# Four u tile buffers and a new order of loads, one-hots and selections in a one-core encoder step

## The reference

```
x += W_o [ headRMS(DiffAttn(x_n)) ; headRMS(StickBreak(x_n)) ]
h  = x;  xb = RMSNorm(h)                       # feed-forward part, "PEER"
q  = (xb @ w_q) as 8 heads x 2 halves x 128    # scores against 128 sub keys per half
top 16 of each half, top 16 of the 256 sums  -> 16 experts per head, gate = softmax
y  = sum over 128 chosen experts of gelu(u[e] . xb) * gate * v[e]
```

## Time and profile before

| what | value |
|---|---|
| time, median of 3 runs | 2113.67 us (2110.81 to 2116.14) |
| the profiled execution's own time | 2118.96 us |
| its span, first to last instruction | 2117.2 us, 25395 instructions |
| mean granted TensorE clock | 0.958 |
| PE busy | 1952.6 us, 92% |
| DVE busy | 1276.0 us, 60% |
| ACT busy | 653.5 us, 31% |
| POOL busy | 516.1 us, 24% |
| DMA | 484.30 MB, mean 229 GB/s |
| chain that ended last | PE 57%, DMA 20%, DVE 13%, ACT 6%, issue 3% |

### The profile page before, as it was taken

How to read it: one execution, slowest core, us unless ns; L and a number is a source line. 1 busy time by engine, 2 the same in 40 slices (tenths; PEclk the granted TensorE clock), 3 DMA queues, 4 the chain that set the end, 5 groups by cost and what they waited for, 6 DMA issues and landing times.

```text
span 2117.2 us, 25395 instructions
## 1 busy us (share of the span) xinstructions
PE 1952.6 (92%) x9365; PEld 1470.9 (69%) x9365; DVE 1276.0 (60%) x2475; ACT 653.5 (31%) x1392; POOL 516.1 (24%) x408
## 2 busy tenths in 40 slices
PE   6999899999999898998898989779999999999997
PEld 6998665589998788887887888764444444444443
DVE  3113775633767676888998778554545554465456
ACT  3223564433444333335676667220000000000001
POOL 0001100000000121222122223444444444354441
PEclk9999798779999999999999999889999999999999
DMA  5223000002123687776777788989999999999996
GB/s 193 85 81 130 24 1 1 1 23 70 61 81 117 213 264 254 261 246 209 236 252 244 261 300 303 367 304 360 354 375 353 360 379 343 375 371 336 386 351 228
DMA packets 168351, 484.30 MB, mean 229 GB/s; under 512 B 15200, under 2 KB 72544, under 8 KB 164528
## 3 DMA queue, kind: packets, MB, share of 16 engines
q1 hardware_dynamic: 111280, 270.92, 35.9%
q0 software_dynamic: 56528, 208.28, 27.5%
q10 hardware_dynamic: 432, 3.64, 0.4%
HBM read 422.61 MB, written 59.90 MB: 228 GB/s over the span
## 4 chain that ended last, share of the span: by engine, by line
PE 57%; DMA 20%; DVE 13%; ACT 6%; issue 3%; SPq 1%; POOL 0%; ACTq 0%; DVEq 0%; POOLq 0%
PE ps L903 23%; DMA raw<-w_tiles 11%; PE ps L555 10%; PE ps L884 7%; PE ps L822 5%; DMA g_in<-gates_scattered 4%; DMA act_in<-activated 4%; DVE w_lo L1176 3%; DVE hot L1518 3%; PE ps L649 3%; ACT hot L1114 2%; ACT w_hi L1138 2%; PE ps L573 2%; PE ps L640 1%; PE ps L690 1%
## 5 line engine op out<-in xcount | busy, mean ns | idle before, releaser
L903 PE MATMUL ps<-v_buf,p_ring 128*128 128x512 f32 x1536 | 662.4, 593 | 17.3 <-DVE p_ring L1583 14.7
L903 PEld LDWEIGHTS ps<-v_buf,p_ring 128*128 128x128 f32 x1536 | 291.1, 190 | 388.0 <-issue 363.8
L884 PE MATMUL ps<-md_hi,w_hi 128*128 128x384 f32 x1024 | 367.5, 359 | 61.2 <-DVE w_lo L1176 59.9
L1176 DVE TENSOR_TENSOR w_lo<-raw,w_hi 128x1024 fp32r<-128x1024 f32 x176 | 215.5, 1224 | 329.6 <-ACT w_hi L1138 182.6
L884 PE MATMUL ps<-md_lo,w_hi 128*128 128x384 f32 x1024 | 351.5, 343 | 0.0
L884 PE MATMUL ps<-md_hi,w_lo 128*128 128x384 f32 x1024 | 351.2, 343 | 0.0
L535 POOL DMA_INDIRECT ring<-u_rows,idx_a x128 | 173.7, 1357 | 598.5 <-DVE dots L1536 478.1
L1583 DVE TENSOR_TENSOR p_ring<-act_in,g_in 128x384 f32<-128x384 f32 x128 | 70.6, 553 | 318.0 <-DMA act_in<-activated 208.5
L884 PEld LDWEIGHTS ps<-md_hi,w_hi 128*128 128x128 f32 x1024 | 199.3, 195 | 77.4 <-DVE w_lo L1176 76.4
L1544 DVE SCALAR_TENSOR_TENSOR acc<-ring,actg,acc 128x1024 f32<-128x1024 f32 x188 | 232.9, 1277 | 0.8 <-DMA ring<-v_rows,idx_a 0.8
L1536 DVE CUSTOM_DVE_ANT_0 ring<-ring,x_n 128x1024 f32<-128x1024 f32 x192 | 230.0, 1220 | 1.8
(11 more groups left out here) (230 smaller groups left out, 2509.4 us busy)
## 6 DMA issues: line engine op xcount, KB each, us to landing
raw<-w_tiles SPq DMA_DIRECT2D x176, 512.0 KB, 5.3
v_buf<-v_rows SPq DMA_DIRECT2D x128, 512.0 KB, 8.4
activated<-act_st SPq DMA_DIRECT2D x128, 192.0 KB, 2.6
gates_scattered<-g_st SPq DMA_DIRECT2D x24, 1024.0 KB, 5.0
g_in<-gates_scattered SPq DMA_DIRECT2D x32, 768.0 KB, 15.4
act_in<-activated SPq DMA_DIRECT2D x32, 768.0 KB, 12.0
kv_t<-qkv ACTq DMA_DIRECT2D x3, 1184.0 KB, 7.5
xh<-x_t SPq DMA_DIRECT2D x8, 296.0 KB, 13.2
```

The source lines that it names most:

```text
L884: mm = nc.tensor.matmul(ps[:, slot, 0:ND], w[:, slot, kc, :], x[:, kc, :], start=(kc == 0 and j == 0), stop=(kc == KC - 1 and j == 2))
L903: mm = nc.tensor.matmul(ps[:, 2 + 2 * t + h, :], p_ring[:, i % 3, t * P:(t + 1) * P], v_buf[i % V_SLOTS][:, 512 * h:512 * h + 512], start= ...
L1176: TT(w_lo[:, slot], raw[:, slot], w_hi[:, slot].bitcast(F32), SUB).then_inc(w_split, 1)
```

## The change

- `raw_u`: four buffers for u tiles. The two new ones lie where buffers 5 and 6 of the ring were, so the ring has 5 buffers for the first 139 gathers (`RING_U`, `RING_AT`) and 7 after; the first use of buffers 5 and 6 waits for the end of the u stage (`u_done`).
- `load_u`: SP issues the load of tile i+4, not i+2, at the head of tile i's turn. The first loads of the new buffers wait for the last sub-key scores (`sc_done`).
- DVE's order per tile is one-hots, remainder, step, dots; ACT's is cast, scaling, copies, gelu.
- `act_dram` holds four tiles side by side, so `load_acts` reads 6 KB per partition in one row; the stores stay 1.5 KB per partition.
- Six selections of D2 move into the query stage, one in each of its last six tiles (`D2_EARLY`). Three "sel" steps fewer remain (74 steps, not 77), and `STEP_LINE` has 54 steps before tile 64, not 55. The exponents now stand at tiles 8, 31, 49, 66 and 89.

```diff
-SEL_STEPS, TOP_STEPS = {RT_B: 4, RT_D2: 8}, 13
+D2_EARLY = 6
+SEL_STEPS, TOP_STEPS = {RT_B: 4, RT_D2: (16 - D2_EARLY) // 2}, 13
-STEP_LINE = [(0, 0), (9, 13), (64, 55), (90, N_STEPS)]
+STEP_LINE = [(0, 0), (9, 13), (64, 54), (90, N_STEPS)]
-RING = 7
+RING_U, RING_V, RING_AT = 5, 7, U_DOTS
+RAW_SLOTS = 4
-    act_dram = nc.dram_tensor("activated", (N_EXP * P, ND), F32).ap()
+    act_dram = nc.dram_tensor("activated", (N_EXP // 4 * P, 4 * ND), F32).ap()
+        raw_u = [raw[:, 0], raw[:, 1]] + [at(f"raw{k}", [P, KC, P], F32, region + 8192 + 4096 * (k - 2))[:] for k in (2, 3)]
-        def ring_slot(s):
-
-            return ring[s % RING][:], gath_in[s % RING], 16 * (s // RING + 1)
+        ring_slots, last_use, landings = [], [None] * RING_V, [0] * RING_V
+        for op in range(N_OPS):
+            k = op % RING_U if op < RING_AT else (op - RING_AT) % RING_V
+            landings[k] += 1
+            ring_slots.append((k, 16 * landings[k], last_use[k]))
+            last_use[k] = op
...
             def load_acts(grp):
-                sp.dma_start(act_in[:, grp % 2], act_dram[4 * grp * P:4 * (grp + 1) * P, :].rearrange(
-                    "(j p) t -> p j t", p=P)).then_inc(act_in_s[grp % 2], 16)
+                sp.dma_start(act_in[:, grp % 2].rearrange("p j t -> p (j t)"),
+                             act_dram[grp * P:(grp + 1) * P, :]).then_inc(act_in_s[grp % 2], 16)
...
+            def load_u(i):
+                if i < RAW_SLOTS:
+                    sp.wait_ge(sc_done, N_PQ)
+                else:
+                    sp.wait_ge(w_split, B_U + i - RAW_SLOTS + 3)
+                sp.dma_start(raw_u[i % RAW_SLOTS], w_tiles[(B_U + i) * P:(B_U + i + 1) * P, :]).then_inc(
+                    raw_in[i % RAW_SLOTS], 16)
+
+            for i in range(2, RAW_SLOTS):
+                load_u(i)
             for i in range(N_EXP):
-                if i + 2 < N_EXP:
-                    load_tile(B_U + i + 2, i % 2)
+                if i + RAW_SLOTS < N_EXP:
+                    load_u(i + RAW_SLOTS)
...
-                if s >= RING:
-                    pool.wait_ge(gath_used, s - RING + 1)
+                if before is not None:
+                    pool.wait_ge(gath_used, before + 1)
+                if before is None and slot >= RING_U:
+                    pool.wait_ge(u_done, N_EXP)
...
+                for g in groups_of(i, 0):
+                    scale_hots(g)
                 for g in groups_of(i, 1):
                     take_gates(g)
-                for g in groups_of(i, 0):
-                    scale_hots(g)
...
                     select([(s, u - 1) for s in EARLY])
+                if u >= N_PQ - D2_EARLY:
+                    select([(RT_D2, u - N_PQ + D2_EARLY)])
...
             for i in range(N_EXP):
+                for g in groups_of(i, 0):
+                    one_hot(g)
                 if i + 1 < N_EXP:
-                    lo_part(B_U + i + 1, (i + 1) % 2)
+                    lo_part(B_U + i + 1, (i + 1) % 2, raw_u[(i + 1) % RAW_SLOTS])
```

More of the change, by code:

```diff
@@ L236, in bass_hybrid_step @@
         ring_off = [m0_off + 2 * KC * ND * 4 + 4096 * k for k in range(3)] + [region + 4096 * k for k in range(4)]
-        ring = [at(f"ring{k}", [P, D], F32, ring_off[k]) for k in range(RING)]
+        ring = [at(f"ring{k}", [P, D], F32, ring_off[k]) for k in range(RING_V)]
+        raw_u = [raw[:, 0], raw[:, 1]] + [at(f"raw{k}", [P, KC, P], F32, region + 8192 + 4096 * (k - 2))[:] for k in (2, 3)]
         mq_hi = at("mq_hi", [P, KC, TQ], F32R, region)
@@ L314, in bass_hybrid_step @@
         tables_in, caches_in = sem("tables_in"), sem("caches_in")
-        raw_in = [sem("raw_in0"), sem("raw_in1")]
+        raw_in = [sem(f"raw_in{k}") for k in range(RAW_SLOTS)]
         hi_ready = sem("hi_ready")
@@ L347, in bass_hybrid_step @@
         idx_ready = sem("idx_ready")
-        gath_in = [sem(f"gath_in{k}") for k in range(RING)]
+        gath_in = [sem(f"gath_in{k}") for k in range(RING_V)]
         gath_used, gl_done, gl_gated = sem("gath_used"), sem("gl_done"), sem("gl_gated")
@@ L441, in _ @@
                 sp.wait_ge(act_done, i + 1)
-                sp.dma_start(act_dram[i * P:(i + 1) * P, :], act_st[:, i % 4]).then_inc(act_stored[i % 4], 16)
+                sp.dma_start(act_dram[i // 4 * P:(i // 4 + 1) * P, i % 4 * ND:(i % 4 + 1) * ND],
+                             act_st[:, i % 4]).then_inc(act_stored[i % 4], 16)
                 if i == G_AT + 2:
@@ L530, in _ @@
                     pool.wait_ge(idx_ready, 2)
-                dst, landed, _ = ring_slot(s)
-                if s >= RING:
-                    pool.wait_ge(gath_used, s - RING + 1)
+                slot, _, before = ring_slots[s]
+                if before is not None:
+                    pool.wait_ge(gath_used, before + 1)
+                if before is None and slot >= RING_U:
+                    pool.wait_ge(u_done, N_EXP)
                 idx = idx_b[:, k:k + 1] if blk else idx_a[:, k:k + 1]
-                pool.indirect_dma_start(dst, None, u_rows if table == "u" else v_rows,
-                                        bass.IndirectOffsetOnAxis(ap=idx, axis=0)).then_inc(landed, 16)
+                pool.indirect_dma_start(ring[slot][:], None, u_rows if table == "u" else v_rows,
+                                        bass.IndirectOffsetOnAxis(ap=idx, axis=0)).then_inc(gath_in[slot], 16)
         @block.tensor
@@ L1132, in _ @@
                 if i + 1 < N_EXP:
-                    act.wait_ge(raw_in[n % 2], 16 * (n // 2 + 1))
+                    k = (i + 1) % RAW_SLOTS
+                    act.wait_ge(raw_in[k], 16 * ((B_U // 2 if k < 2 else 0) + (i + 1) // RAW_SLOTS + 1))
                     if i == 0:
@@ L1137, in _ @@
                         act.wait_ge(u_done, i)
-                    nc.scalar.copy(w_hi[:, n % 2], raw[:, n % 2]).then_inc(hi_ready, 1)
+                    nc.scalar.copy(w_hi[:, n % 2], raw_u[k]).then_inc(hi_ready, 1)
                 if 1 <= i <= 10:
@@ L1172, in _, with lo_part @@
             TT, TS = nc.vector.tensor_tensor, nc.vector.tensor_scalar
-            def lo_part(n, slot):
+            def lo_part(n, slot, src=None):
                 dve.wait_ge(hi_ready, n + 1)
-                TT(w_lo[:, slot], raw[:, slot], w_hi[:, slot].bitcast(F32), SUB).then_inc(w_split, 1)
+                TT(w_lo[:, slot], raw[:, slot] if src is None else src, w_hi[:, slot].bitcast(F32), SUB).then_inc(w_split, 1)
             def factors(name, w, r=1):
@@ L1480, in routing @@
                         for k in range(SEL_STEPS[s]):
-                            select([(s, 2 * k), (s, 2 * k + 1)])
+                            h0 = 2 * k + (D2_EARLY if s == RT_D2 else 0)
+                            select([(s, h0), (s, h0 + 1)])
                             yield None
@@ L1524, in gathered @@
                 table, blk, k = OPS[s]
-                rows, landed, n = ring_slot(s)
+                slot, n, _ = ring_slots[s]
+                rows = ring[slot][:]
                 if s == 0:
@@ L1533, in gathered @@
                     dve.wait_ge(gl_gated, 1)
-                dve.wait_ge(landed, n)
+                dve.wait_ge(gath_in[slot], n)
                 if table == "u":
@@ L1563, in _ @@
                     normed_rows()
-                for g in groups_of(i, 0):
-                    one_hot(g)
                 for _ in range(along(STEP_LINE, i), along(STEP_LINE, i + 1)):
```

## The result

The changed kernel took **2019.07 us** (median of 4 runs, 2013.59 to 2027.12), the kernel before 2114.9 us in the runs beside it (median of 4, 2110.81 to 2117.15). Between the two profiled executions (2118.96 and 2013.59 us) the difference is 105.4 us.

A forecast was written before the change was run, and what follows sets the result against it. PE was 92% busy, with 120 us of the u stage not its own work, mainly late loads and scaling. Terms 15 + 18 + 14 + 7 + 3 = 57 us gave 2057 us for the median, range 2032 to 2085 us.

The forecast's parts named there:

- the corner where everything works at once: Whole kernel: every part reaches its upper end; left out of the range, with two rivals, together less than 0.2.
- First stretch: Tiles 12 to 63: four u buffers remove most pauses from late loads, -15 us, bounds 8 and 22.
- Second stretch: Tiles 64 to 89: new orders and three steps fewer, with DVE the limit, -18 us, bounds 6 and 27.
- Third stretch: Tiles 90 to 111: one-hots ahead and loads on time remove PE's pauses, -14 us, bounds 8 and 20.
- Last stretch: Tiles 112 to 127: limited by transfers at some 365 GB/s, -7 us, bounds 0 and 18.
- Rows of 6 KB: V stage: longer rows for activations land little sooner, -3 us of 0 to 14.7.
- New waits: Waits added by `load_u`, the first loads and POOL's wait for the u stage's end: 0 us.
- Selections in the query stage: Query stage: six moved selections fit into DVE's waits for ACT's scores, 0 us; without that cover 10 us.
- DVE did not take the loads' place: Rival, first two stretches: pauses and idle time come back as DVE's, gain 38 us, 2076 us; chance 0.17.
- the rival with 0.12: V stage: longer pieces get more of the engines and pauses go, -14.7 instead of -3, 2045 us; chance 0.12.
- The ring of five did not starve DVE: Rival, last two stretches: five gather buffers starve DVE, slower, 2131 us at 20 us landing; chance 0.03.
- Loads did come earlier: Denies the rival that transfers limit the u stage and two more buffers only queue, 2086 us; chance 0.06.

The follow-up runs named there:

- early preload: The changed kernel with gate pieces issued at v tiles 1, 3, 5, 7 and 3.1 MB of v-stage preloads moved to tiles 94 to 106; 2000.26 us.
- ring of three: The changed kernel with three gather buffers in the u stage instead of five; 2022.75 us, one run.

## Why the prediction came out as it did

The direction and each place were right; every size was too small. The 2019.07 us lie 13 us below the range's lower end and 7 us above what all upper ends together gave (2012 us): the range left out "the corner where everything works at once", and nearly that corner came. Between the profiled executions the gain passed the sum of 57 us by 48: 12 in the first stretch, 13 in the third, 9 in the last, 5 in the second, 4 in the v stage and 6 ahead of tile 12. The first and the third term passed even their own upper bounds, 22 and 20 us.

- **First stretch, −15 forecast, −26.6 measured: mis-sized.** The step that failed is "I take 15, nearer to the pauses counted". The pauses were counted well (−14.1), but PE's busy time fell by 12.5 us more, where the forecast had "some 2 us of slow matmuls". In the earlier trace rows it was there to be read: 52 tiles at 4.16 us are 216 us, against 230.1 us busy. The granted clock accounts for at most some 7 us of it (0.97 to 1.00 on 230 us, an estimate); that the rest are starts held back too little to be listed is an inference. The kernel before with 6 KB rows, with the same code in this stretch, fits it: its clock was 0.99 there, and PE was busy 228.0 us all the same. The forecast's own 216 us for the 52 tiles was nearly reached, so 31.5 us were to be had, and the deduction for late remainders by DVE was not needed: DVE is busy 187.9 of 221.2 us, and PE waits for it 3.6 us.
- **Second stretch, −18 and −22.9: right in kind, near in size.** DVE's work was forecast as 163.7 us and is 165.1, at 96% busy. The stretch is 5 us shorter than assumed (171.4 for 176), with less idle time of DVE. Undone one at a time, the selections cost 7.4 us there, the two orders 14.9, two of the buffers 4.8.
- **Third stretch, −14 and −26.5: the failed step is the floor, "26 x 6.2 = 161" and "22 x 6.2 = 136" as what "PE alone would need".** 6.20 us was the loop of ACT and DVE; with that open the pace is 6.00, and there each gelu does wait for PE. The upper bound of 20 us was therefore no bound. With the loads in time the old order still kept nearly every tile at 6.20 us, without one wait of PE for the remainder or the scaling.
- **Last stretch, −7 and −16.2: the rule was right, its rate too low.** The bytes set the end, as early preload showed, but at 386 GB/s, not "some 365 GB/s". The 18 us of the upper bound were nearly reached. The failed step is the scaling of the v stage's mean by its busy share, which did not give the rate at full use (355 GB/s at 0.96 are 370, not 365, but that is worth 1 us only). How the 16.2 us divide is open: two buffers fewer cost 10.0 us in the changed kernel, and 6 KB rows alone came with 10.6 in the kernel before.
- **Rows of 6 KB, −3 and, by themselves, −14.1 to −27.7: failed.** The step is "longer rows of the kind that v already has were no faster". It compared two loads' landing times at different sizes. The same 768 KB landed in 12.0 us with 1.5 KB rows and in 9.3 us with 6 KB rows, in the kernel before with that edit. Why they land sooner is not shown; they run beside the gathers, in a stage with engines 96% busy. That the stage as a whole came within 5 us of its term is luck: this gain, taken too small, and a new pause, taken for nothing, partly cancel. The Trainium skill (DMA: Bandwidth & Descriptors, section Specifications) has the line rate from 512 B on; by that rule the edit gives nothing, and the runs do not agree with it: 14.1 us in one kernel, 19.9 in another. The Trainium skill (same page, section Queues, rings and completion order), which the rival drew on, has each engine take turns between queues packet by packet. That fits the sign if longer rows make a larger turn, which no run here shows.
- **New waits, 0: failed at one place.** The forecast looked at `load_u` and the ring, not at SP's four gate pieces ahead of the v loads. They held SP 22.03 us and PE 9.4 us. Why they held SP 8 us longer than before is open, but for the ring's part in it; the edit that spreads them removes the pause.
- **Selections in the query stage, 0: right.** The tiles of that stage stay 7.81 us apart, and in a tile with one more selection DVE's wait for the scores falls from 2.54 to 0.83 us, near the 1.66 us that the forecast had for it.
- **The rivals.** DVE did not take the loads' place. The v stage did lose its pauses for products, the rival with 0.12, though the stage gave only half of that back. The ring of five did not starve DVE: its waits for gathers sum to 1.1 us in the last two stretches. Loads did come earlier: ACT's waits for them, 64.1 us in the first stretch, are gone there.

## What to carry to other kernels

Judge a stretch by its length less the pace of an undisturbed tile, not by the waits listed in it: an engine that is fed late also stretches its busy time, by a lower clock and by starts held back too little to be listed. Before calling a steady pace an engine's own, follow one period through every engine that takes part; if each step starts when the one before ends, the pace is a loop, and an order that opens it is worth trying, with both ends of the loop moved together. When a stage gets shorter, look again at which transfers stand in one queue behind which, and try longer rows for a load that the stage waits for.

## What the runs showed of the hardware

- Transfers of several queues moved 386 GB/s on average over 86.8 us and 384 GB/s over 78.3 us, at a busy share of 1.01 and 1.00; the last two lines of the earlier trace rows had 339 and 355 GB/s at 0.94 and 0.96.
- Row length changed the v stage by 14.1 and 19.9 us at the same bytes, with gathers in 4 KB rows running beside it.
- Four transfers of 768 KB held SP's queue 13.84, 14.82, 22.03 and 22.89 us in four kernels (before, ring of three, the change, the change with short rows), and all that stood behind them with it.
- The clock granted before the u stage differs from run to run with the same code there. In the windows from 200 to 300 us of the change and of the change with short rows it was 0.86 and 0.74, between the two levels of 1.2 and 2.4 GHz, and the first gelu came at 652.0 and 666.6 us:

```profile
200.00:300.00 100.00, 95.63 (x528) 68.52 (x526) 76.25 (x163) 59.56 (x136) 13.67 (x11) 0.86 0.11 46
```

```profile
200.00:300.00 100.00, 92.64 (x445) 65.67 (x444) 67.95 (x138) 50.96 (x114) 13.20 (x13) 0.74 0.12 47
```

That is why one run of a kernel here says little about 10 us, and a stretch of its u stage, where loads are in time, says much about 1 us.
